# First slab behind each adaptive norm: products on h times the feature scale, token scale and shift applied in the bank afterwards

## The chip, the cores and the metric

The kernel runs on one NeuronCore of a Trainium2 chip. The metric is device time in microseconds of one execution. One core has five engines that run their own instruction streams and wait for each other by semaphores: TensorE (PE, matmul; its weight loads are PEld in the profile), VectorE (DVE), ScalarE (ACT), GpSimd (POOL) and SyncE (SP, which issues the transfers).

## The reference

Two transformer blocks run one after the other on x of 512 tokens by 1024 features, in float32. The first block has retention, forgetting attention, a cross attention to a memory and a gated feed-forward part. The second block is adaptive; what matters here is its two norms:

```
mod = silu(c) @ w_ada + b_ada;  sh1, sc1, g1, sh2, sc2, g2 = split(mod, 6)
h = rmsnorm(x, norm1_g) * (1.0 + sc1) + sh1
proj = h @ w_in                       # pool input, k, v, q
x = x + g1 * (concat(attention, pool_mixer) @ w_out)
h2 = rmsnorm(x, norm2_g) * (1.0 + sc2) + sh2
x = x + g2 * conv_gated_ffn(h2, w_up, conv_w, conv_b, w_down)
```

rmsnorm divides each token by the root of the mean of its squares over the 1024 features. So a projection behind a norm is: token scale times (weights times (h times feature scale)) plus weights times shift.

## The kernel before, in words

Everything lies with features on the 128 partitions and the 512 tokens along the free dimension, so h is 8 tiles h[:, k, :] of 128 x 512. A weight matrix is cut into slabs of 8 x 128 input features by 256 outputs (1 MB). Each float32 product is made of three products of a reduced form (fp32r): whi*xhi, whi*xlo, wlo*xhi, where xhi is the rounded value and xlo the rest. A slab has 8 k, 2 output tiles and 3 parts: 48 matmuls of 128 x 512 (three() and slab_fm(), L1366 to L1387).

A slab passes four engines. SyncE loads it into raw[s] (two buffers, s = slab number mod 2), once wlo of the slab before is made. ScalarE rounds it to whi[s] (make_hi, L408) when TensorE is done with the slab that had this buffer (slab_done). GpSimd subtracts to wlo[s] in four quarters (L388) and counts wlo_ready. TensorE waits for wlo_ready and for a pair of result banks (pair_free), and writes lin banks in turn. The results are evicted by ScalarE or VectorE.

The order of every engine is written out by hand. Around each adaptive norm it is as follows. The slabs of "down" (before norm1) or "out2" (before norm2) give four pairs of tiles; residual() on VectorE adds each to h (L1118 or L1120), residual_act() on ScalarE squares the new h (L680), and accumulate() on VectorE sums the squares in rstd (L859, L863). Then token_norm() on TensorE: one filler product into a free bank (keep_clock, L1424; a float32 product is two instructions), eight one-column products that sum the squares of each block of 128 tokens (L1433), one filler, and, when ScalarE has taken the root (L428) and VectorE the reciprocal and the scaled diagonals in tmp[0] (L872, L875), four products that spread the token scale over a bank, att[1] (L1439); then three fillers. finish_norm() then works in both engines per k: VectorE makes tmp = h * feature scale * att[1] (L887), ScalarE adds the shift and rounds to xh (L432), VectorE makes the rest xl (L881). TensorE starts k of the first slab when xl of k is there (ready, then k outside and the two tiles inside). ScalarE rounds the second slab behind the norm between the root and this loop (beside). 

Behind norm1 comes "in2" (L1735 on): ScalarE, after the loop, waits for pool["u"] (VectorE's two memsets, L1226), evicts the first slab's pair (pool_in, L744) and only then rounds the third slab (make_hi). VectorE makes window sums for the pool mixer (L1240 to L1250). Behind norm2 comes "ffn2" as a hardware loop: VectorE copies the convolution's parameters (L1325), ScalarE evicts the first slab's pair (L829), then rounds the third slab (L833), and so on.

Before norm1, VectorE also sums up the modulation (ada tiles, L1175) beside "down"; modulation() (L1207, L1211) makes the feature scales after the third pair.

## Time and profile before

| | us |
|---|---|
| median of 3 runs | 1402.72 |
| lowest, highest | 1400.03, 1402.81 |
| the profiled execution | 1399.9 |
| its span, first to last instruction | 1398.1 |
| TensorE busy | 1361.8 (97%) |
| VectorE busy | 660.2 (47%) |
| ScalarE busy | 619.4 (44%) |
| GpSimd busy | 613.9 (44%) |

Times in the profile are microseconds from the start of the span. A row of the timeline gives start, duration, engine, line of the kernel, operation, tile written and tiles read, and how often; in brackets stands how long the engine was idle before and who ended that. Merged rows (x2, x4) give the duration of the whole group. A TensorE matmul is pipelined: its duration overlaps the next, so the step is read from start to start.

### The profile page before, as it was taken

To read this page: it belongs to the slowest core of one execution; us is meant where nothing else is said; L and a number is where in the kernel's file an instruction comes from. 1 tells how busy PE (TensorE), PEld (TensorE's weight loads), DVE (VectorE), ACT (ScalarE), POOL (GpSimd) and SP (SyncE) were. 2 spreads that over 40 slices of the span, in tenths; PEclk is the share of its full clock that TensorE was granted. 3 is DMA by queue.
4 is the path that set the end of the run, shared out by engine and by line. 5 is a ranking of instruction groups with operands and counts; after the bars stand their busy time and mean duration, and the time that the engine had idled before them with its cause. 6 is when DMAs were issued, how large, how long until landed. Compare 5 with 4: busy or idle time off the path is not lost.

```text
span 1398.1 us, 17303 instructions
## 1 busy us (share of the span) xinstructions
PE 1361.8 (97%) x6544; PEld 1095.2 (78%) x6544; DVE 660.2 (47%) x973; ACT 619.4 (44%) x861; POOL 613.9 (44%) x448
## 2 busy tenths in 40 slices
PE   9999999999989999999999999988999999999999
PEld 7877955788876888888888887854878888888887
DVE  5434938355433444344343316588255555554111
ACT  5555228553444443434442123587245545554111
POOL 3444320374430456555564543411325555556453
PEclk9999999999999999999999999999999999999999
DMA  7222212142220244344436433200312222323422
GB/s 267 91 90 94 87 41 81 61 173 99 91 90 1 91 144 141 135 159 141 150 135 260 177 135 105 91 31 30 121 61 90 90 90 92 118 90 135 175 96 90
DMA packets 29055, 155.23 MB, mean 111 GB/s; under 512 B 3024, under 2 KB 4176, under 8 KB 14800
## 3 DMA queue, kind: packets, MB, share of 16 engines
q1 hardware_dynamic: 29008, 154.57, 31.5%
q8 instruction: 34, 0.56, 0.2%
q14 instruction: 13, 0.11, 0.0%
HBM read 152.46 MB, written 2.10 MB: 111 GB/s over the span
## 4 chain that ended last, share of the span: by engine, by line
issue 39%; PE 30%; POOL 26%; DVE 4%; DMA 0%; POOLq 0%; ACT 0%; SPq 0%
POOL wlo L388 26%; PE lin L1368 10%; PE lin L1370 10%; PE lin L1369 10%; DVE small L1026 1%; DVE expd L1037 1%; DMA raw<-w_slabs 0%; PE lin L1571 0%; DVE xl L906 0%; DVE win L1245 0%; DVE small L1030 0%; POOLq L397 0%; DVE wlo L914 0%; PE att L1433 0%; PE att L1439 0%
## 5 line engine op out<-in xcount | busy, mean ns | idle before, releaser
L388 POOL TENSOR_TENSOR wlo<-raw,whi 128x512 fp32r<-128x512 f32 x444 | 613.7, 1413 | 768.8 <-ACT whi L415 508.2
L1368 PE MATMUL lin<-xh,whi 128*128 128x512 f32 x1072 | 420.6, 392 | 4.0 <-POOL wlo L388 3.5
L1370 PE MATMUL lin<-xh,wlo 128*128 128x512 f32 x1072 | 417.6, 390 | 0.0
L1369 PE MATMUL lin<-xl,whi 128*128 128x512 f32 x1072 | 417.4, 389 | 0.0
L415 ACT ACTIVATE whi<-raw 128x2048 fp32r<-128x2048 f32 x66 | 126.6, 1918 | 266.7 <-PE lin L1370 260.4
L1368 PEld LDWEIGHTS lin<-xh,whi 128*128 128x128 f32 x1072 | 201.3, 188 | 52.5 <-issue 5.9
L1370 PEld LDWEIGHTS lin<-xh,wlo 128*128 128x128 f32 x1072 | 201.3, 188 | 42.1
L1369 PEld LDWEIGHTS lin<-xl,whi 128*128 128x128 f32 x1072 | 201.3, 188 | 41.4 <-issue 0.5
L1368 PE MATMUL lin<-fh,whi 128*128 128x512 f32 x352 | 137.1, 390 | 0.0
L1370 PE MATMUL lin<-fh,wlo 128*128 128x512 f32 x352 | 137.0, 389 | 0.0
L1369 PE MATMUL lin<-fl,whi 128*128 128x512 f32 x352 | 137.0, 389 | 0.0
L1368 PEld LDWEIGHTS lin<-fh,whi 128*128 128x128 f32 x352 | 66.1, 188 | 14.0 <-issue 0.3
L1370 PEld LDWEIGHTS lin<-fh,wlo 128*128 128x128 f32 x352 | 66.1, 188 | 13.6
L1369 PEld LDWEIGHTS lin<-fl,whi 128*128 128x128 f32 x352 | 66.1, 188 | 13.6
L1175 DVE CUSTOM_DVE_ANT_0 adar<-adar,c_act 128x1024 f32<-128x1024 f32 x48 | 57.9, 1215 | 38.9 <-DMA adar<-ada 38.6
L1120 DVE SCALAR_TENSOR_TENSOR h<-lin,mod,h 128x512 f32<-128x512 f32 x16 | 11.9, 751 | 118.8 <-PE lin L1370 118.8
L1331 DVE SCALAR_TENSOR_TENSOR tmp<-lin,convp,tmp 128x511 f32<-128x511 f32 x44 | 31.2, 750 | 68.4 <-ACT tmp L829 68.4
L728 ACT ACTIVATE whi<-raw 128x2048 fp32r<-128x2048 f32 x22 | 42.2, 1919 | 40.6 <-PE lin L1370 40.5
L1118 DVE TENSOR_TENSOR h<-lin,h 128x512 f32<-128x512 f32 x24 | 16.4, 691 | 86.5 <-PE lin L1370 86.4
L1184 DVE TENSOR_TENSOR tmp<-lin,rstd 128x512 f32<-128x512 f32 x22 | 15.2, 692 | 83.7 <-PE lin L1370 83.5
L1368 PE MATMUL lin<-xah,whi 128*128 128x512 f32 x128 | 50.6, 395 | 0.0
L1370 PE MATMUL lin<-xah,wlo 128*128 128x512 f32 x128 | 49.9, 390 | 0.0
(320 smaller groups left out, 1925.5 us busy)
## 6 DMA issues: line engine op xcount, KB each, us to landing
raw<-w_slabs SPq DMA_DIRECT2D x111, 1024.0 KB, 4.8
adar<-ada SPq DMA_DIRECT2D x48, 512.0 KB, 5.5
h<-x_t SPq DMA_DIRECT2D x4, 512.0 KB, 6.4
decay<-decay SPq DMA_DIRECT2D x4, 512.0 KB, 7.9
out_t<-h SPq DMA_DIRECT2D x3, 512.0 KB, 8.2
raw<-w_slabs SPq DMA_DIRECT2D x4, 256.0 KB, 7.0
rope<-rope SPq DMA_DIRECT2D x2, 512.0 KB, 7.3
memx<-mem_t SPq DMA_DIRECT2D x1, 1024.0 KB, 5.9
```

Of the source, the lines that this page charges most:

```text
L388: return nc.gpsimd.tensor_tensor(wlo[s][:, ks, :], raw[s][:, ks, :], f(whi[s][:, ks, :]), ALU.subtract)
L415: nc.scalar.activation(whi[g % 2][:, :, :], raw[g % 2][:, :, :], ACT.Copy).then_inc(whi_ready, 1)
L728: nc.scalar.activation(whi[s][:, :, :], raw[s][:, :, :], ACT.Copy).then_inc(whi_ready, 1)
L1026: last = nc.vector.tensor_reduce(ring(j, "max")[:, e:e + 1], att[n % 4][:, 0:width(j)], AX.X, ALU.max, negate=True)
L1037: nc.vector.tensor_scalar(row, row, ring(j - 1, "inverse")[:, e:e + 1], None, ALU.mult).then_inc(a["norm"], 1)
L1118: ins = nc.vector.tensor_tensor(h[:, k, :], b[:, :], h[:, k, :], ALU.add)
L1175: return nc.vector.tensor_tensor_reduce(adar[s][:, :], adar[s][:, :], c_act[:, :], 1.0, 0.0, ALU.mult, ALU.add, total).then_inc(ada["acc"], 1)
L1184: nc.vector.tensor_tensor(tmp[s][:, :], lin[2 * p][:, :], rstd[:, :], ALU.mult).then_inc(ffn["g"], 1)
L1331: nc.vector.scalar_tensor_tensor(t[:, 1:T], b[:, 0:T - 1], convp[s][:, 4 * j:4 * j + 1], t[:, 1:T], ALU.mult, ALU.add).then_inc(ffn2["tap" ...
L1368: nc.tensor.matmul(out, whi_, xhi_, start=first, stop=False)
L1369: nc.tensor.matmul(out, whi_, xlo_, start=False, stop=False)
L1370: return nc.tensor.matmul(out, wlo_, xhi_, start=False, stop=last)
```

## The change

The token scale is one factor per token, so it can be applied after the product. The first slab behind each adaptive norm is therefore multiplied with sch and scl, the high and low part of h times the feature scale, which need no token scale. For norm1 they use the memory of xh and xl (so ScalarE waits for scaled["read"] before it overwrites a tile), for norm2 free memory.

- ScalarE makes sch tiles: six in a row and the two shift copies before the last pair of "down" (norm1), or two per pair of "out2" (norm2); the last two always behind the last adds. VectorE makes scl tiles: for norm1 six behind modulation(), before the add of the last pair, and two behind the last add; for norm2 two per pair.
- TensorE's scaled_slab() replaces token_norm() and the first slab. The eight token sums stand before k = 3 and the four diagonal products before k = 6. Behind the last k stand 32 products of the 16 weight tiles (whi and wlo, two output tiles each) with a two-column operand, the high and low part of the shift. The five fillers of each norm (one, one, three) are gone.
- ScalarE rounds the second slab first, then takes the root, then copies the bank att[1] to rstd; VectorE's L887 reads rstd in place of the bank.
- VectorE's fix_slab(), within finish_norm behind k = 5, waits for the first slab, adds the two columns of the shift products, multiplies both banks in place by rstd and adds the shift sums. ScalarE (and in ffn2 VectorE) waits for scaled["fixed"] before it evicts.
- The semaphores of the second gated part are shared with the first (ffn2 uses ffn's), with offsets of FT.

```diff
+            def scaled_hi(i, k):
+                nc.scalar.activation(sch[i][:, k, :], h[:, k, :], ACT.Copy, scale=gain(i, k)
+                                     ).then_inc(scaled["hi"], 1)
             def finish_norm(n, hi, shift, beside):
+                beside()
                 act.wait_ge(n["sum"], 1)
                 nc.scalar.activation(token_root, att[0][:, 0:TT], ACT.Sqrt, bias=ccol(C_EPS)).then_inc(n["sd"], 1)
-                beside()
+                act.wait_ge(n["sum"], 2)
+                nc.scalar.activation(rstd[:, :], att[1][:, :], ACT.Copy).then_inc(n["sd"], 1)
                 for k in range(KT):
+                    if n is norms["norm1"]:
+                        act.wait_ge(scaled["read"], k + 1)
                     act.wait_ge(n["x"], k + 1)
...
@@ residual_act
+                    if norm == 0 and u == 3:
+                        act.wait_ge(ada["mod"], 1)
+                        for i in range(2):
+                            nc.scalar.activation(shift_hl[i][:, :, 0], mod[:, 3 * i * KT:(3 * i + 1) * KT], ACT.Copy
+                                                 ).then_inc(ada["shift"], 1)
+                        for k in range(6):
+                            scaled_hi(0, k)
...
+                        if norm == 1 or norm == 0 and u == 3:
+                            scaled_hi(norm, k)
...
@@ VectorE
+            def scaled_lo(i, u):
+                for k in range(2 * u, 2 * u + 2):
+                    dve.wait_ge(scaled["hi"], KT * i + k + 1)
+                    nc.vector.scalar_tensor_tensor(scl[i][:, k, :], h[:, k, :], gain(i, k), f(sch[i][:, k, :]),
+                                                   ALU.mult, ALU.subtract).then_inc(scaled["lo"], 1)
+            def fix_slab(i, p):
+                dve.wait_ge(slab_done, SLAB0["in2" if i == 0 else "ffn2"] + 1)
+                parts = att[0][:, 8:12].rearrange("p (j e) -> p j e", e=2)
+                link(nc.vector.tensor_reduce(slab_shift[i][:, :], parts, AX.X, ALU.add))
+                banks = lin[2 * (p % 2):2 * (p % 2) + 2]
+                for b in banks:
+                    last = nc.vector.tensor_tensor(b[:, :], b[:, :], rstd[:, :], ALU.mult)
+                link(last)
+                for j, b in enumerate(banks):
+                    nc.vector.tensor_scalar(b[:, :], b[:, :], slab_shift[i][:, j:j + 1], None, ALU.add
+                                            ).then_inc(scaled["fixed"], 1)
...
                 for k in range(KT):
                     if k >= 4:
                         dve.wait_ge(n["lo"], k - 3)
-                    nc.vector.scalar_tensor_tensor(tmp[k % 4][:, :], h[:, k, :], gain(k), att[1][:, :],
+                    nc.vector.scalar_tensor_tensor(tmp[k % 4][:, :], h[:, k, :], gain(i, k), rstd[:, :],
                                                    ALU.mult, ALU.mult).then_inc(n["x"], 1)
                     if k >= 1:
                         low(k - 1)
+                    if k == 5:
+                        fix_slab(i, p)
...
@@ beside_down on VectorE
                 if u == 2:
                     modulation()
+                    for i in range(2):
+                        dve.wait_ge(ada["shift"], 2)
+                        nc.vector.tensor_tensor(shift_hl[i][:, :, 1], mod[:, 3 * i * KT:(3 * i + 1) * KT],
+                                                f(shift_hl[i][:, :, 0]), ALU.subtract).then_inc(ada["shift"], 1)
+                    for v in range(3):
+                        scaled_lo(0, v)
...
@@ TensorE
+            def scaled_slab(i, name):
+                n, g, p = norms[f"norm{i + 1}"], SLAB0[name], PAIR0[name]
+                s, banks = g % 2, lin[2 * (p % 2):2 * (p % 2) + 2]
+                pe.wait_ge(wlo_ready, g + 1)
+                pe.wait_ge(pair_free, p + 1)
+                for k in range(KT):
+                    if k == 3:
...
+                                pe.wait_ge(made, count)
+                                mm = nc.tensor.matmul(att[0][:, t:t + 1], part[:, P * t:P * (t + 1)], ccol(C_MEAN_D),
+                                                      start=(e == 0), stop=(e == 1))
+                        mm.then_inc(n["sum"], 1)
+                    if k == 6:
+                        for t in range(TT):
+                            pe.wait_ge(n["inv"], t + 1)
+                            mm = nc.tensor.matmul(att[1][:, P * t:P * (t + 1)], mean_d, tmp[0][:, P * t:P * (t + 1)],
+                                                  start=True, stop=True)
+                        mm.then_inc(n["sum"], 1)
+                    pe.wait_ge(scaled["lo"], KT * i + k + 1)
+                    for j in range(2):
+                        mm = three(banks[j][:, :], whi[s][:, k, j * P:(j + 1) * P], wlo[s][:, k, j * P:(j + 1) * P],
+                                   sch[i][:, k, :], scl[i][:, k, :], k == 0, k == KT - 1)
+                    if i == 0:
+                        mm.then_inc(scaled["read"], 1)
+                pe.wait_ge(ada["shift"], 4)
+                for j in range(2):
+                    for e, w in enumerate((whi, wlo)):
+                        for k in range(KT):
+                            mm = nc.tensor.matmul(att[0][:, 8 + 2 * j:10 + 2 * j], w[s][:, k, j * P:(j + 1) * P],
+                                                  shift_hl[i][:, k, :], start=(e == 0 and k == 0), stop=(e == 1 and k == KT - 1))
+                mm.then_inc(slab_done, 1)
```

## Rows read from the trace of the kernel before

**Rows 1.** TensorE in the timeline around norm1 (start, us, engine, line, operation)

```profile
845.76 1.02 PE L1424 MATMUL c_act<-con 128*128 128x512 f32 x2
...
856.92 0.79 PE L1368 MATMUL lin<-xh,whi 128*128 128x512 f32 x1
...
868.25 0.39 PE L1368 MATMUL lin<-xh,whi 128*128 128x512 f32 x1
...
879.13 0.39 PE L1368 MATMUL lin<-xh,whi 128*128 128x512 f32 x1
```

**Rows 2.** TensorE's waits: who waited for whom, us in total, times, longest

```profile
PE lin L1368 <- POOL wlo L388: 4.9, 6, 1.4
```

**Rows 3.** TensorE in the timeline around norm2

```profile
1022.96 1.02 PE L1424 MATMUL c_act<-con 128*128 128x512 f32 x2
...
1025.76 0.36 PE L1433 MATMUL att<-con,rstd 128*128 128x1 f32 x2
1025.98 0.36 PE L1433 MATMUL att<-con,tmp 128*128 128x1 f32 x2
...
1027.76 1.92 PE L1439 MATMUL att<-tmp,con 128*128 128x128 f32 x8
...
1044.22 0.39 PE L1368 MATMUL lin<-xh,whi 128*128 128x512 f32 x1
...
1055.18 0.49 PE L1368 MATMUL lin<-xh,whi 128*128 128x512 f32 x1
```

**Rows 4.** ScalarE in the timeline around norm1

```profile
837.86 1.92 ACT L415 ACTIVATE whi<-raw 128x2048 fp32r<-128x2048 f32 x1 [8.96 <-PE lin L1370]
...
847.31 0.63 ACT L680 ACTIVATE tmp<-h 128x512 f32<-128x512 f32 x1 [4.00 <-DVE h L1118]
...
868.50 1.08 ACT L744 ACTIVATE upool<-lin 128x512 f32<-128x512 f32 x2 [3.44 <-PE lin L1370]
```

**Rows 5.** GpSimd in the timeline around norm1

```profile
839.85 5.47 POOL L388 TENSOR_TENSOR wlo<-raw,whi 128x512 fp32r<-128x512 f32 x4 [5.86 <-ACT whi L415]
...
871.47 6.66 POOL L388 TENSOR_TENSOR wlo<-raw,whi 128x512 fp32r<-128x512 f32 x4 [13.66 <-ACT whi L415]
```

**Rows 6.** ScalarE in the timeline behind norm2

```profile
1044.48 1.28 ACT L829 ACT_TABLE_LOAD   x1 [3.28 <-PE lin L1370]
```

**Rows 7.** GpSimd in the timeline behind norm2

```profile
1049.11 5.93 POOL L388 TENSOR_TENSOR wlo<-raw,whi 128x512 fp32r<-128x512 f32 x4 [15.16 <-ACT whi L833]
```

**Rows 8.** VectorE in the timeline behind norm2

```profile
1029.71 1.41 DVE L887 SCALAR_TENSOR_TENSOR tmp<-h,mod,att 128x512 f32<-128x512 f32 x2 [1.94 <-PE att L1439]
1031.25 1.56 DVE L881 SCALAR_TENSOR_TENSOR xl<-tmp,mod,xh 128x512 fp32r<-128x512 f32 x1
...
1040.37 1.62 DVE L881 SCALAR_TENSOR_TENSOR xl<-tmp,mod,xh 128x512 fp32r<-128x512 f32 x2
```

**Rows 9.** The page's groups: busy us, mean ns of one, idle before

```profile
L1184 DVE TENSOR_TENSOR tmp<-lin,rstd 128x512 f32<-128x512 f32 x22 | 15.2, 692 | 83.7 <-PE lin L1370 83.5
```

**Rows 10.** VectorE in the timeline around norm1

```profile
841.95 0.69 DVE L1118 TENSOR_TENSOR h<-lin,h 128x512 f32<-128x512 f32 x1 [24.84 <-PE lin L1370]
...
853.88 1.41 DVE L887 SCALAR_TENSOR_TENSOR tmp<-h,mod,att 128x512 f32<-128x512 f32 x2 [2.24 <-PE att L1439]
...
864.22 1.62 DVE L881 SCALAR_TENSOR_TENSOR xl<-tmp,mod,xh 128x512 fp32r<-128x512 f32 x2
...
873.60 1.68 DVE L1245 TENSOR_TENSOR win<-win 128x525 f32<-128x525 f32 x1
```

**Rows 11.** Stretches of 1 us: busy us per engine, then PEclk, DMA share, GB/s

```profile
849.00:850.00 1.00, 1.00 (x7) 1.00 (x6) 0.00 (x0) 0.00 (x0) 0.00 (x0) 0.51 1.07 275
...
855.00:856.00 1.00, 1.00 (x2) 0.34 (x1) 0.87 (x2) 1.00 (x2) 1.00 (x1) 0.57 0.08 33
...
1026.50:1027.50 1.00, 1.00 (x2) 0.27 (x1) 0.78 (x5) 1.00 (x2) 0.00 (x0) 0.51 0.00 0
...
1029.50:1030.50 1.00, 1.00 (x3) 0.50 (x3) 0.79 (x2) 0.01 (x1) 1.00 (x2) 0.78 0.00 0
```

More of the change, by code:

```diff
@@ L266, in build @@
         ffn = sems("ffn", "g act y hi lo")
-        ffn2 = sems("glu2", "pc cv tap act f hi lo")
-        ada = sems("ada", "act acc mod")
+        ffn2 = dict(ffn, **sems("glu2", "pc cv tap"))
+        scaled = sems("scaled", "hi lo read fixed")
+        ada = sems("ada", "act acc mod shift")
         pool = sems("pool", "u pooled hi lo mm")
@@ L733, in _ @@
                                          tmp[2 + s][:, :], ACT.Copy).then_inc(ffn["hi"], 1)
-            residual_act("down", norms["norm1"], 3)
+            residual_act("down", norms["norm1"], 3, norm=0)
             finish_norm(norms["norm1"], xhi, 0, lambda: make_hi(SLAB0["in2"] + 1))
@@ L742, in pool_in @@
                 act.wait_ge(pair_free, p + 2)
+                if u == 0:
+                    act.wait_ge(scaled["fixed"], 2)
                 for j in range(2):
@@ L817, in _ @@
                         beside_gqa_act, late=2)
-            residual_act("out2", norms["norm2"])
+            residual_act("out2", norms["norm2"], norm=1)
             finish_norm(norms["norm2"], xhi, 3 * KT, lambda: make_hi(SLAB0["ffn2"] + 1))
+            act.wait_ge(scaled["fixed"], 4)
             with act.Fori(0, FT // 2) as i:
@@ L867, in accumulate, with finish_norm @@
                         ins.then_inc(n["acc"], 1)
-            def finish_norm(n, gain, hi, lo, shift):
+            def scaled_lo(i, u):
[14 more added lines that the diff above has]
+                                            ).then_inc(scaled["fixed"], 1)
+            def finish_norm(i, hi, lo, p):
+                n, shift = norms[f"norm{i + 1}"], 3 * i * KT
                 dve.wait_ge(n["sd"], 1)
@@ L1092, in _, with residual @@
                                             ).then_inc(xkn["out"], 1)
-            def residual(name, n, scale=None, slabs_per_pair=1, split=None, beside=None, before=None):
+            def residual(name, n, scale=None, slabs_per_pair=1, split=None, beside=None, before=None, norm=None):
                 def low(u):
@@ L1130, in residual @@
                         beside(u)
+                if norm is not None:
+                    scaled_lo(norm, 3)
                 if split is not None:
@@ L1219, in beside_down @@
                     modulation()
+                    for i in range(2):
[4 more added lines that the diff above has]
+                        scaled_lo(0, v)
             tiles_beside_down(0)
-            residual("down", norms["norm1"], slabs_per_pair=3, beside=beside_down)
-            finish_norm(norms["norm1"], lambda k: mod[:, KT + k:KT + k + 1], xhi, xlo, shift=0)
+            residual("down", norms["norm1"], slabs_per_pair=3, beside=beside_down, norm=0)
+            finish_norm(0, xhi, xlo, PAIR0["in2"])
             link(nc.vector.memset(upool[:, :, 0:PAD], 0.0))
@@ L1317, in _ @@
             softmax_dve(gqa, 16, 4, lambda j: T, True, gqa_lo, beside_gqa_dve, late=2)
-            residual("out2", norms["norm2"], scale=lambda k: mod[:, 2 * KT + k:2 * KT + k + 1])
-            finish_norm(norms["norm2"], lambda k: mod[:, 4 * KT + k:4 * KT + k + 1], xhi, xlo, shift=3 * KT)
+            residual("out2", norms["norm2"], scale=lambda k: mod[:, 2 * KT + k:2 * KT + k + 1], norm=1)
+            finish_norm(1, xhi, xlo, PAIR0["ffn2"])
+            dve.wait_ge(scaled["fixed"], 4)
             with dve.Fori(0, FT // 2) as i:
@@ L1692, in _, with down @@
             project("ffn", slab_fm, first=2)
-            def down(name, parts):
+            def down(name, made):
                 g, p = SLAB0[name], PAIR0[name]
@@ L1732, in _ @@
             g, p = SLAB0["in2"], PAIR0["in2"]
-            for u in range(5):
+            for u in range(1, 5):
                 pe.wait_ge(wlo_ready, g + u + 1)
                 pe.wait_ge(pair_free, p + u + 1)
-                mm = slab_fm(u % 2, p + u, ready=(lambda k: pe.wait_ge(norms["norm1"]["lo"], k + 1)) if u == 0 else None,
+                mm = slab_fm(u % 2, p + u, ready=(lambda k: pe.wait_ge(norms["norm1"]["lo"], k + 1)) if u == 1 else None,
                              middle=(lambda: head_stats(2 * (u - 3))) if u >= 3 else None)
```

56 lines of the change are left out of this document (27 added, 29 removed).

## The prediction

> **What bounds the kernel now.** I read the page's busy shares first, then TensorE's waits, then the timeline around the two adaptive norms, engine by engine. TensorE is busy 97% of the span, and the split products run back to back: 48 of them, one slab, go from 868.25 to 879.13, so one takes 0.2267 us [rows 1]. What TensorE waits for by name is small: the longest total behind a slab product is 4.9 us in 6 waits, all on GpSimd's low part of the weights [rows 2]. But in two places its stream holds norm work and filler products that no wait shows. Call the slabs behind a norm A, B and C. Behind norm1 the next product could issue at 845.76 and A starts at 856.92; B starts at 868.25, where 845.76 + 10.88 would be 856.64: 11.6 us lost. Behind norm2 B starts at 1044.22, where 1022.96 + 10.88 is 1033.84: 10.4 us lost [rows 1, 3]. These 22 us are what the change can win.
>
> The reader must also see how C comes to start, since it needs whi and wlo in the buffer that A leaves. ScalarE rounds C's weights only after finish_norm's last high part, and after it has evicted A; GpSimd follows. Behind norm1 the eviction starts at 868.50, and GpSimd ends C's low part at 871.47 + 6.66 = 878.13; TensorE wants it at 879.13: slack 1.0 us [rows 1, 4, 5]. Behind norm2 the table load before the eviction starts at 1044.48, GpSimd ends at 1049.11 + 5.93 = 1055.04, and C starts at 1055.18 after B's last product: slack zero [rows 3, 6, 7]. So a later end of finish_norm on VectorE and ScalarE moves C, whatever TensorE does before it.
>
> **The change, norm2 (the simpler one).** TensorE: A's first three k (18 products, 4.1 us) run from 1022.96 to 1027.0. Then the eight token sums: a matmul of one column is two instructions, and two instructions took 0.22 us (1025.98 less 1025.76), so 1.8 us, to 1028.8 [rows 3]. Three more k: to 1032.9. Then the four diagonal products, eight instructions: 1.92 us at the lower clock [rows 3], half of it at the full one, 1.0: to 1033.9. Here is the core of my argument: before, they ran at 1027.76 and VectorE's first x (L887) began at 1029.71 [rows 3, 8]. Now A's products stand ahead of them. ScalarE must also copy the bank to rstd (0.6, the half of 1.08 and an issue, [rows 4]), so x begins at 1034.8: 5.1 later.
>
> VectorE's loop of 16 operations took 12.3 us from there (1040.37 + 1.62 less 1029.71, [rows 8]), but its first low part stood beside GpSimd and took 1.56, where two operations clear of it take 1.41, a step of 0.67 [rows 8]. Now GpSimd has converted B's weights at 1027 to 1033, so the loop is 16 such steps and the first wait for ScalarE: 11.1, a gain of 1.2. In it stands fix_slab, behind low(4): a small reduction, two multiplications and two additions over a bank. The nearest row is 0.692 for a bank times rstd [rows 9]; with two links I take 3.1 (2.7 to 3.4). Its wait for A costs nothing: TensorE ends A and the shift products by 1040.3, low(4) ends about 1042.4. Behind the wait stand x(6) and low(5), and behind these TensorE's last k of B. Sum: 5.1 - 1.2 + 3.1 = 7.0; the last low part ends at 1049.0, then convp's copy (0.17), on which the table load and the eviction wait. They start at 1049.25 instead of 1044.48: +4.8, and rounding and GpSimd follow unchanged. C starts at 1059.95. B, from 1040.3, is done at 1051.2, so TensorE stands idle some 8.7 us.
>
> The 32 shift products of two columns cost TensorE 32 x 0.11 = 3.6 us if they go like those of one column [rows 3], and 7.3 at most, at a full product each [rows 1]. Either way they are hidden: they only shorten that idle time. The five filler products go, and with them what kept TensorE in work while it waits.
>
> **Norm1.** Three things are added. (a) VectorE was idle 24.84 us before the add at 841.95 [rows 10]. Now it waits there for ScalarE's shift copies, behind the rounding of A's weights that ends at 839.8 [rows 4], and then makes six low parts. Four fall beside GpSimd's conversion from 839.85 [rows 5], where an operation with two SBUF inputs took 1.68 [rows 10] instead of 0.66 to step; so they end near 848.5, and GpSimd's own four grow to 4 x 1.66 (its 6.66 for four beside VectorE, [rows 5]): A can start at 846.5 only. The add of h[6] ends at 849.2 instead of 842.6, then three accumulations (2.1), the add of h[7] at 852.0, a scaled high part and the square on ScalarE (0.65 each, by the square's 0.63, [rows 4]): squares complete at 853.3, where before it was 847.9. TensorE has done three k at 850.6 and waits 2.7. (b) The sums end at 855.1, three k at 859.2, the diagonals at 860.2, x begins at 861.1 instead of 853.88. (c) The clock. The granted clock fell to 0.50 (1.2 GHz) from 849.0 to 855.9, after TensorE had waited and issued one-column products, and again at 1026.5 [rows 11]. Now the same thin stretch, with a longer wait, stands in the middle of A; I take 1.7 us for products that run at the lower level (0 to 4). Then +7.2 + 1.7 = 8.9 for x; the loop 0.9 shorter (no GpSimd beside it), fix_slab 3.1, and C's slack and the early end of the loop (865.84 and the memsets to 866.1, against the eviction at 868.50) take off 2.4 + 1.0. C starts 7.7 later, at 886.8; B is done by 879.
>
> **The clock at C.** In both places TensorE now stands idle 7 to 9 us before C. The trace has no idle stretch this long in mid kernel, but shorter thin ones were followed by low stretches of 6.9 and 3.4 us [rows 11]; half of 3.4 is lost if C begins in one: 1.7 each, bounds 0 and 3.4. By the Trainium skill, "TensorE: Matmul & The Clock Gate", section "Part 1: The HAM clock gate", the throttled level is the default and only activity releases it; that speaks against this change, and the rows on the granted clock agree. Without that rule the sum would be some 5 us smaller (the three clock terms).
>
> **Sum.** Norm1 7.7 + 1.7 = 9.4; norm2 4.8 + 1.7 = 6.5; together 16. From C on all engines are late alike, and the stages that follow hang on one another (slab to slab on TensorE, softmax after it), so I expect nothing back. Elsewhere the edit is free: the scaled parts of k 0 to 5 before norm2 fall into idle time of both engines between residual adds, and no DMA moves: the next weight loads wait only on wlo_ready, up to 3 us later against more than 10 of lead. The profiled execution took 1399.9 (span 1398.1), the median of the runs is 1402.72, the lowest 1400.03; 1399.9 + 16 = 1415.9, and 1417 with part of that difference.
>
> **The rivals.** *No clock loss:* everything as above without the three clock terms: +10.9, 1411 to 1413. For it: in stage norm2 the one-column products now have full ones on both sides. Against: the idle time before C is longer than any before. 22%.
>
> *The other side, TensorE's fill decides:* if ScalarE and VectorE were done in time, the change would win at B. A costs 10.9 + 1.8 + 1.0 + 3.6 (shift), plus 3.5 of waits at norm1: B at 866.5 against 868.25, and at 1040.3 against 1044.22; together -5.7, so 1394 to 1397. It decides fully from the point where C's low part is ready when B ends (877.4 and 1051.2), so where the eviction of A starts by 867.8 and 1040.6; the time is below that of before as soon as finish_norm ends no later than it did. Both need it 7 to 9 us earlier than I have it, or C's rounding ahead of the eviction. For it speaks only that 22 us lie open; I see nothing in the order of the instructions that does it. 8%.
>
> *GpSimd beside the loop:* x now reads rstd in SBUF instead of the bank, so each of its operations has two SBUF inputs. If B's weights are converted during the loop, four operations step 1.66 instead of 0.66: +4 at one norm or both, 1420 to 1425. For it: x began beside GpSimd before. Against: B's rounding is moved ahead of the root and GpSimd is done before x begins. By the skill's "SBUF — State Buffer", section "SBUF: two separate sides", such an operation and one of GpSimd exclude each other for their whole length; the 1.68 us rows agree, and by that rule x would be exposed. 8%.
>
> **How the numbers follow.** The forecast, 62%: 1417, own range 1411 to 1423 (clock terms 0 to 9, fix_slab, the stalls of norm1). With the rivals the range is 1407 to 1425. 0.2% is 2.8 us, about what a measurement of this kernel tells from no change. Faster 8% (the rival of the other side), the same 3% (my sums wrong by 13 us in between), slower 89%.
>
> **What would show it.** In the profile after: x begins near 1034.8 after norm2, not at 1029.7; TensorE's waits on wlo L388 grow from 4.9 to about 20 us, in two long ones before C; the eviction of A waits on VectorE, not on TensorE; the granted clock is 0.5 at the start of C; B starts earlier than before. Wrong would be a C that starts without a wait, or a clock that stays at 1.0 throughout, or a B that is itself late.

## The result: slower by 1.1%

| | before | after |
|---|---|---|
| median us | 1401.43 | 1415.11 |
| runs, lowest to highest | 4, 1400.03 to 1402.81 | 4, 1414.43 to 1416.34 |
| the profiled execution | 1399.9 | 1415.01 |
| its span | 1398.1 | 1412.9 |
| mean granted clock | 0.994 | 0.987 |

The ratio is 1.0107, 95% interval 1.009 to 1.0123. The forecast was 1417 (1407 to 1425).

TensorE's waits in the profile after (who waited for whom, total us, times, longest), the row that answers to [rows 2]:

```profile
PE lin L1434 <- POOL wlo L400: 16.3, 8, 5.7
```

Two waits of 5.7 and 5.6 us are new, and both are C's. TensorE's timeline behind norm1 and norm2 after, answering to [rows 1, 3]; the bracket is the idle time and who ended it:

```profile
845.75 0.47 PE L1434 MATMUL lin<-xh,whi 128*128 128x512 f32 x1
...
852.84 0.38 PE L1501 MATMUL att<-con,tmp 128*128 128x1 f32 x2 [1.49 <-ACT tmp L711]
...
855.54 0.77 PE L1434 MATMUL lin<-xh,whi 128*128 128x512 f32 x1
...
861.82 1.05 PE L1507 MATMUL att<-tmp,con 128*128 128x128 f32 x8
...
865.47 0.95 PE L1520 MATMUL att<-shift_hl,whi 128*128 128x2 f32 x8
...
868.96 0.48 PE L1434 MATMUL lin<-xh,whi 128*128 128x512 f32 x1
...
887.45 0.79 PE L1434 MATMUL lin<-xh,whi 128*128 128x512 f32 x1 [5.70 <-POOL wlo L400]
...
1032.91 0.39 PE L1434 MATMUL lin<-sch,whi 128*128 128x512 f32 x1
...
1050.05 0.49 PE L1434 MATMUL lin<-xh,whi 128*128 128x512 f32 x1
...
1068.43 0.79 PE L1434 MATMUL lin<-xh,whi 128*128 128x512 f32 x1 [5.61 <-POOL wlo L400]
...
1080.97 0.39 PE L1434 MATMUL lin<-xh,whi 128*128 128x512 f32 x1
```

A now starts at once: 845.75 instead of 856.92. B starts 0.7 later than before at norm1 (in this profile; see the first experiment), and 4.1 earlier at norm2 (1050.05 less 1044.22 is +5.8, but norm2 as a whole begins 9.95 later). Then C is 8.3 later at norm1 and, with the 9.95 taken off, 3.3 later at norm2. The slab behind C, D, shows the clock as well: it starts 13.76 and 12.54 behind C, where before it was 12.09 and 11.02. In sum D is +10.0 and then +4.8, which is the 14.8 us of the span. Up to the last product of down, from the fifth slab behind norm1 to the last product of out2, and from the fifth slab behind norm2 to the end the two profiles differ by less than 0.2 us each. So A's head start was there, and it was lost, and more, at C.

Who holds C is on the other engines. VectorE after norm1, answering to [rows 10]: the six low parts, the add of h[6], the diagonals, the x loop's first operations, the bank operations within it and the end of the loop:

```profile
841.00 7.18 DVE L905 SCALAR_TENSOR_TENSOR xl<-h,mod,xh 128x512 fp32r<-128x512 f32 x6
848.11 0.68 DVE L1173 TENSOR_TENSOR h<-lin,h 128x512 f32<-128x512 f32 x1
...
856.22 3.69 DVE L928 TENSOR_SCALAR tmp<-con,small 128x128 f32<-128x128 f32 x4
863.54 1.42 DVE L940 SCALAR_TENSOR_TENSOR tmp<-h,mod,rstd 128x512 f32<-128x512 f32 x2 [3.63 <-ACT rstd L447]
...
871.12 0.15 DVE L912 TENSOR_REDUCE slab_shift<-att 128x2 f32<-128x4 f32 x1
871.30 1.30 DVE L915 TENSOR_TENSOR lin<-lin,rstd 128x512 f32<-128x512 f32 x2
872.64 1.42 DVE L918 TENSOR_SCALAR lin<-lin,slab_shift 128x512 f32<-128x512 f32 x2
873.96 0.74 DVE L940 SCALAR_TENSOR_TENSOR tmp<-h,mod,rstd 128x512 f32<-128x512 f32 x1
...
876.88 0.75 DVE L934 SCALAR_TENSOR_TENSOR xl<-tmp,mod,xh 128x512 fp32r<-128x512 f32 x1 [0.19 <-ACT xh L453]
```

The x loop starts 9.66 us later than before, and the bank operations hold it for 2.84 (873.96 less 871.12). Behind it stand ScalarE's eviction of A and the rounding of C, then GpSimd's low part, answering to [rows 4, 5]:

```profile
877.87 1.09 ACT L777 ACTIVATE upool<-lin 128x512 f32<-128x512 f32 x2 [1.02 <-DVE upool L1292]
878.84 1.92 ACT L427 ACTIVATE whi<-raw 128x2048 fp32r<-128x2048 f32 x1
```

```profile
880.84 6.56 POOL L400 TENSOR_TENSOR wlo<-raw,whi 128x512 fp32r<-128x512 f32 x4 [21.20 <-ACT whi L427]
```

The eviction used to wait for TensorE's product; now it waits for VectorE, 9.4 us later. Norm2 after, on ScalarE, GpSimd and VectorE, answering to [rows 6, 7, 8]:

```profile
1057.10 0.72 ACT L453 ACTIVATE xh<-tmp,mod 128x512 fp32r<-128x512 f32 x1 [0.60 <-DVE tmp L940]
1057.84 1.28 ACT L862 ACT_TABLE_LOAD   x1
1059.14 1.45 ACT L862 ACTIVATE tmp<-lin,convp 128x512 f32<-128x512 f32 x2
```

```profile
1062.47 5.83 POOL L400 TENSOR_TENSOR wlo<-raw,whi 128x512 fp32r<-128x512 f32 x4 [20.42 <-ACT whi L866]
```

```profile
1044.64 1.42 DVE L940 SCALAR_TENSOR_TENSOR tmp<-h,mod,rstd 128x512 f32<-128x512 f32 x2 [2.31 <-ACT rstd L447]
...
1056.98 1.63 DVE L934 SCALAR_TENSOR_TENSOR xl<-tmp,mod,xh 128x512 fp32r<-128x512 f32 x2
1058.53 0.16 DVE L1391 COPY convp<-par 128x8 f32 x1
```

The table load stands right behind ScalarE's last high part, before VectorE's copy to convp at 1058.53 is made. The clock when C begins, in stretches of 1 us (busy us per engine, then PEclk, DMA share, GB/s):

```profile
886.00:887.00 1.00, 0.00 (x0) 0.00 (x0) 0.96 (x2) 0.00 (x0) 1.00 (x1) 0.50 0.00 0
...
888.00:889.00 1.00, 1.00 (x4) 0.76 (x3) 0.90 (x2) 1.00 (x2) 0.00 (x0) 0.50 0.54 74
...
1070.00:1071.00 1.00, 1.00 (x4) 0.81 (x3) 1.00 (x2) 1.00 (x1) 0.00 (x0) 0.50 0.75 287
```

TensorE idles at 0.50 and starts C at 0.50.

### The profile page after: what moved, and what is told of

It is laid out like the page before. It is cut to its first block, busy times and chain, and to the rows that moved or that the text cites. A ratio compares the mean times of both kernels' runs of the same rounds, so it can differ in the third digit from the quotient of the medians.

```text
span 1412.9 us, 17468 instructions
## 1 busy us (share of the span) xinstructions
PE 1366.1 (97%) x6588; PEld 1103.8 (78%) x6588; DVE 681.0 (48%) x1001; ACT 630.9 (45%) x881; POOL 613.6 (43%) x448
## 4 chain that ended last, share of the span: by engine, by line
issue 47%; POOL 28%; PE 24%; DMA 0%; DVE 0%; POOLq 0%; SPq 0%; ACT 0%
POOL wlo L400 28%; PE lin L1434 8%; PE lin L1435 8%; PE lin L1436 8%; DMA raw<-w_slabs 0%; DVE xl L961 0%; POOLq L409 0%; DVE wlo L969 0%; POOLq L412 0%; SPq L299 0%; DVE h L1175 0%; ACT xh L468 0%; SPq L305 0%; SPq L301 0%; POOLq L404 0%
## 5 line engine op out<-in xcount | busy, mean ns | idle before, releaser
L1434 PE MATMUL lin<-xh,whi 128*128 128x512 f32 x1056 | 418.0, 396 | 14.8 <-POOL wlo L400 14.8
L1434 PEld LDWEIGHTS lin<-fh,whi 128*128 128x128 f32 x352 | 66.1, 188 | 14.1 <-issue 0.3
L759 ACT ACTIVATE whi<-raw 128x2048 fp32r<-128x2048 f32 x22 | 42.2, 1920 | 40.5 <-PE lin L1436 40.4
L1243 DVE TENSOR_TENSOR tmp<-lin,rstd 128x512 f32<-128x512 f32 x22 | 15.2, 692 | 83.7 <-PE lin L1436 83.5
L1435 PE MATMUL lin<-xal,whi 128*128 128x512 f32 x128 | 49.8, 389 | 0.0
```

Source lines behind the costliest of these rows:

```text
L759: nc.scalar.activation(whi[s][:, :, :], raw[s][:, :, :], ACT.Copy).then_inc(whi_ready, 1)
L1243: nc.vector.tensor_tensor(tmp[s][:, :], lin[2 * p][:, :], rstd[:, :], ALU.mult).then_inc(ffn["g"], 1)
L1434: nc.tensor.matmul(out, whi_, xhi_, start=first, stop=False)
L1435: nc.tensor.matmul(out, whi_, xlo_, start=False, stop=False)
```

## The experiments

The theory: the time is lost where C waits for its weights' low part, because everything between the norm's sums and C's rounding stands in one order, and the sums now come later; the clock adds to it when C starts cold. Times below are medians; a ratio is to the kernel before, run beside it with a median of 1399.7 to 1400.0, and takes in all runs, so it is not the quotient of the two medians.

**Each norm alone.** Two kernels with a pair of flags: at the norm that is switched off, the old order of products, filler products, rounding and loop stands.

```diff
+ON = (True, False)        # the other kernel: (False, True)
-            scaled_slab(0, "in2")
+            scaled_slab(0, "in2") if ON[0] else token_norm(norms["norm1"])
```

> The change behind norm1 only; norm2 as before (its own first slab, fillers included). My theory (C waits for the late end of finish_norm, then starts at 1.2 GHz): in the profile the first product of the fourth in2 slab stands 10 us later than before (at about 901.2), the stretch behind norm2 is as before, the whole is 10 us over before (ratio 1.007). Rival (the loss is all in the gated part behind norm2, where the kernel is bound by one slab after another): nothing to 2 us over before. Rival (the two losses are not additive, one loss hides in the other): norm1 only plus norm2 only are not the 14 us of the whole.

> The change behind norm2 only; norm1 as before. The scaled parts of norm2 and the two small shift copies stay. My theory: the third ffn2 slab starts 3.3 us later than before relative to the end of out2, and 1.6 us more go by the lower clock: 5 us over before (ratio 1.0035). Rival (the PE's fill decides): 4 us below before, ratio 0.997.

Norm1 alone took 1409.48, ratio 1.0072 (1.0048 to 1.0097); norm2 alone 1407.22, 1.0042 (1.0023 to 1.0062). The two excesses sum to 1.14%, the whole change has 1.07%: within the intervals the norms are independent. Each shows its long wait of C unchanged:

```profile
887.62 0.80 PE L1445 MATMUL lin<-xh,whi 128*128 128x512 f32 x1 [5.74 <-POOL wlo L401]
```

```profile
1061.68 0.79 PE L1445 MATMUL lin<-xh,whi 128*128 128x512 f32 x1 [5.61 <-POOL wlo L401]
```

The first kernel also shows what is particular to the profile of the change. There the granted clock was 0.50 for 6.8 us within A (853.2 to 860.0), and B began 23.6 behind the last product of down (22.7 before). In the profile of norm1 alone, and in four more below with the same instructions up to there, it was 0.50 for 3.4 us within A, and B began 22.0 behind. So the change usually starts B 0.7 earlier at norm1 too; C then stands 40.5 behind that product and D 54.2, against 33.6 and 45.7 before: +6.9 and +8.5, where the profile of the change has +8.3 and +10.0.

**Filler products in the wait.** Eleven 512-column products of the kernel before's keep_clock stand ahead of C at both norms, to hold the clock up and change nothing else.

```diff
             for u in range(1, 5):
+                if u == 2:
+                    keep_clock(11)
                 pe.wait_ge(wlo_ready, g + u + 1)
...
+            keep_clock(11)
             project("ffn2", slab_fm, first=2)
```

> The changed kernel with 11 filler products (float32, 128 x 512, into the free bank) before the third slab behind each norm, in the time in which TensorE waits for GpSimd's low part; nothing else moves. If the low clock at C costs what I said: granted clock 1.0 when C starts, C starts when it did, the fourth slab starts 1.6 us earlier at each norm, together 3.2 us below the changed kernel, some 11.5 us over before (ratio 1.008). If the clock costs nothing of its own (something else is late behind C anyway): as the changed kernel, 14.8 over before. If the fillers themselves delay C: over 15.

It took 1419.72, ratio 1.0142 (1.0118 to 1.0165): 4.6 us above the changed kernel, where I had expected 3 below it. TensorE's row says why (22 instructions for 11 products):

```profile
880.96 9.60 PE L1490 MATMUL c_act<-con 128*128 128x512 f32 x22
...
890.00 0.80 PE L1434 MATMUL lin<-xh,whi 128*128 128x512 f32 x1
...
902.52 0.48 PE L1434 MATMUL lin<-xh,whi 128*128 128x512 f32 x1
```

A filler takes 0.87 us, so eleven overran the wait. Counted from the last product ahead of A, C stands at 42.0 instead of 40.5 at norm1 and at 39.0 instead of 35.8 at norm2. But the question of the clock is answered: C begins at full clock, and D stands 12.52 and 11.31 behind it, where the changed kernel has 13.76 and 12.54. That is 1.2 us at each norm, and it understates the cold start: behind a filler the first step of C is 0.63 us (890.00 to 890.63) instead of 0.23. Against the kernel before (12.09 and 11.02) the cold start costs 1.7 and 1.5. With six fillers:

> The changed kernel with 6 filler products before slab C at each norm. A filler took 0.87 us in the run with 11 (9.6 us together, 2 to 4 us more than the wait they stood in), so 6 take 5.2 us and fit into the 5.6 us of waiting. My theory: C starts at the same time after the end of down and out2 as in the changed kernel, C runs at the full clock, slab D starts 1.2 to 1.6 us earlier at each norm: 2.5 to 3 us below the changed kernel (ratio to before 1.008 or so). Rival (the clock's loss at C is hidden by other engines): D starts as in the changed kernel, ratio 1.010.

It took 1414.52, ratio 1.0102 (1.0085 to 1.0119). Six took 5.31 us; behind norm1 TensorE still waited 2.2 and the clock fell 0.3 us into C (D 13.81 behind it); behind norm2 C ran at full clock with D 10.99 behind it, 1.5 us won. I had expected 2.5 to 3 us for both norms together, and the time is not told apart from that of the changed kernel. So the clock was a small term: the wait has to go, not its coldness.

**Without the bank operations.** The two multiplications and two additions are left out, so the first slab lacks its token scale and shift.

```diff
-                for b in banks:
-                    last = nc.vector.tensor_tensor(b[:, :], b[:, :], rstd[:, :], ALU.mult)
-                link(last)
-                for j, b in enumerate(banks):
-                    nc.vector.tensor_scalar(b[:, :], b[:, :], slab_shift[i][:, j:j + 1], None, ALU.add
-                                            ).then_inc(scaled["fixed"], 1)
+                for j in range(2):
+                    nc.vector.tensor_copy(slab_shift[i][:, j:j + 1], slab_shift[i][:, j:j + 1]
+                                          ).then_inc(scaled["fixed"], 1)
```

> The changed kernel without the two multiplications and two additions of fix_slab over the banks (the wait for A, the small reduction and the counts stay; two copies of one element stand in for them), so the first slab behind each norm misses token scale and shift. My theory: VectorE's chain to the last low part is 2.6 us shorter at each norm and C starts that much earlier, together 5 us below the changed kernel, a little more if the clock falls later (ratio to before 1.006 to 1.007). Rival (fix_slab is hidden beside TensorE's slab B): no change.

It took 1409.53, ratio 1.0062 (1.0045 to 1.0079): 5.6 us less than the changed kernel for two times 2.8 of VectorE. C stood 16.0 and 15.2 behind B instead of 18.5 and 18.4; counted from the last product ahead of A, it is 2.5 us earlier at each norm. So VectorE's chain sets C, nearly one to one.

**C's rounding ahead of the end of the loop.** ScalarE rounds C before the seventh high part instead of behind the eviction of A.

```diff
                 for k in range(KT):
+                    if k == 6 and third is not None:
+                        make_hi(third)
...
-            with act.Fori(0, FT // 2) as i:
+            def gated_pair(i, rounded=False):
...
+            gated_pair(0, rounded=True)
+            with act.Fori(1, FT // 2) as i:
+                gated_pair(i)
```

> The changed kernel with the rounding of slab C moved into finish_norm on ScalarE, ahead of the high part of k = 6, at both norms, where ScalarE is idle 3.4 us behind fix_slab; the eviction of A no longer stands ahead of it. Simple theory (C hangs only on the order of rounding behind finish_norm): C starts when B ends, 5.7 us earlier at each norm and at full clock, together 11 to 14 us below the changed kernel, about 1402. My theory by now: GpSimd then converts beside VectorE's last five operations (steps of 1.66 for 0.66), the last low part and the eviction of A come 4 us later, and the wait moves to slab D, whose rounding stands behind that eviction: C starts 4 to 5 us earlier, D at most 1 to 2 us earlier, together 1 to 4 us below the changed kernel.

It took 1409.63, ratio 1.0066 (1.0044 to 1.0088): 5.5 us better, between the 1 to 4 of my theory and the 11 to 14 of the simple one. Counted from the last product ahead of A, C starts 6.0 us (norm1; 4.4 against norm1 alone, whose A took the same time) and 2.9 (norm2) earlier, but at norm1 the wait turns up one slab later, at D, whose low part GpSimd starts only at 893.67:

```profile
883.45 0.39 PE L1440 MATMUL lin<-xh,whi 128*128 128x512 f32 x1
...
898.82 0.80 PE L1440 MATMUL lin<-xh,whi 128*128 128x512 f32 x1 [3.03 <-POOL wlo L400]
```

Slab E stands where it stood with the change at norm1 alone (67.1 behind the last product of down in both): there, all of it is given back. At norm2 D stays 3.5 earlier.

Another 2.0 us come from something else that the edit does. To round C early behind norm2, it takes the first pass of the gated part out of ScalarE's hardware loop. In every kernel up to here each pass of that loop holds two activation table loads, in this one and in the mended kernels below none; one is left, in the pass that was taken out. The rows are of the kernel before and of the last kernel of this section:

```profile
L829 ACT ACT_TABLE_LOAD  x11: 1283/1283/1283, 1044.5 to 1264.3; - x11
L835 ACT ACT_TABLE_LOAD  x11: 1283/1283/1283, 1049.1 to 1268.9; - x11
```

```profile
L872 ACT ACT_TABLE_LOAD  x1: 1283/1283/1283, 1053.4 to 1053.4; - x1
```

TensorE's slabs in that loop step by 10.96 and 11.02 in turn with the loads and by 10.88 without, which is 1.9 to 2.0 us from the fifth slab behind norm2 to the end of the span. It has nothing to do with the token scale, and the kernel before was not run with it.

**The kernel before, without its five filler products per norm.** What did the change give up by removing them?

```diff
-                keep_clock(1)
-                keep_clock(1)
-                keep_clock(3)
```

> The kernel before without its five filler products behind each adaptive norm. If fillers only keep the clock: slabs A, B, C behind the norm begin at the lower clock for 3 to 6 us, 1 to 3 us over before at each norm (ratio 1.002 to 1.004). If the norm's small products and the wait are thin enough to drop the clock in any case: 0 to 1 us over before, or somewhat below, as the fillers themselves stand in the path (the diagonal products start after one of them).

It took 1403.28, ratio 1.0015 (1.0004 to 1.0026). At norm2 A starts 1.0 earlier without the fillers, but at the lower clock, and B 0.8 later:

```profile
1031.11 2.08 PE L1437 MATMUL att<-tmp,con 128*128 128x128 f32 x8 [0.89 <-DVE tmp L875]
1035.66 0.76 PE L1368 MATMUL lin<-xh,whi 128*128 128x512 f32 x1 [2.47 <-DVE xl L881]
```

At norm1 B came 0.9 earlier, so at the two norms together nothing is lost. What this profile has over that of before, 4.4 us of span, lies ahead of norm1, where the instructions are the same: its last product of down starts at 850.13 instead of 845.53, behind 13.7 us at the clock of 0.50 instead of 3.4. So what the fillers are worth to the old order is not shown.

**The change with its order mended.** The idea is kept. The sums are asked for after two k (one at norm2) and the diagonals after four (three) instead of three and six; ScalarE squares before it makes the scaled part, and takes the root before B's rounding; C's rounding stands ahead of the seventh high part, D's in front of the pooled tiles' parts and of the first silu.

```diff
-                    if k == 3:
+                    if k == (2, 1)[i]:            # the token sums
-                    if k == 6:
+                    if k == (4, 3)[i]:            # the diagonals' products
```

> The change kept, its order mended where my theory puts the loss. Token sums before k = 2 (norm1) or 1 (norm2) and the diagonals before k = 4 or 3; squares ahead of the scaled high parts; at norm1 only one low part ahead of h[6], with the accumulation of the third pair made earlier; ScalarE rounds B behind the root, C ahead of k = 6, D right behind A's eviction (ffn2) or behind B's results, ahead of the pooled tiles (in2). My theory: x begins about 8 to 9.5 us after the end of down and out2 instead of 17 and 12, C starts without a long wait, 3 to 5 us earlier than in the kernel before at each norm, and D is not late: 5 to 9 us below before (ratio 0.994 to 0.997). Rival (the bank work and the second set of parts cost more than the stall of TensorE, in any order): no less than before, ratio 1.000 or over.

It took 1400.87, ratio 1.0001 (0.999 to 1.0011): all 14 us are back, and nothing more, where I had expected 5 to 9 below before. One execution took 1395.58 at a mean clock of 0.998, the one with the profile; most had 0.991 to 0.993. The difference lies in low stretches elsewhere in the kernel: this profile has none ahead of norm1, that of the next kernel has 6.8 us at 251 to 258 and 3.4 us at 411 to 415, and reaches the last product of down 4.0 us later (848.20 against 844.21). So I compare distances between landmarks from here on. C stood 33.3 behind the last product of down (33.6 before) and 31.1 behind that of out2 (32.45).

C's low part had long been made at both norms. At norm2 C waited 1.4 us for A's banks, which VectorE reads last, and B had waited 0.8 for its own last low part. At norm1 it waited for neither: TensorE ran B without a break, but at the clock of 0.50 from 862.9 to 869.7, which cost 3.0 us, and C followed B's last product. The banks were evicted at 875.6. TensorE alone, in a stretch of 2 us (busy us, then PEclk, DMA share, GB/s), and C's first product:

```profile
864.00:866.00 2.00, 2.00 (x6) 0.50 0.00 0
```

```profile
877.51 0.39 PE L1448 MATMUL lin<-xh,whi 128*128 128x512 f32 x1
```

I had not seen this when I wrote the next expectation, which puts both starts of C down to the banks.

**The bank operations later in the loop.** They stand behind the eighth product of x, ahead of the last two low parts, with the memsets of upool behind them.

```diff
+                    if k == 7:
+                        fix_slab(i, p)            # and, at norm1, the two memsets
                     if k >= 1:
                         low(k - 1)
-                    if k == 5:
-                        fix_slab(i, p)
```

> The version with the order mended, and in it the two bank operations moved from behind the sixth high part to behind the eighth product of the x loop (ahead of the last two low parts), at norm1 the two memsets of upool right behind them, and at norm2 the diagonals' products one k step earlier (ahead of k = 2). In the mended version before this, C began 33.3 us behind the last product of down (13.85 us behind B, against 10.9 for 48 products) and 31.1 us behind the last of out2 (13.6 behind B), although C's low part had been done for 4.4 us at norm1 and 5.0 at norm2: it waited for A's banks, which were evicted only behind the last low part, that GpSimd's pass had slowed (1.7 us a step). Theory: with the bank operations and half of the x loop ahead of GpSimd's pass the banks come free in time; B's 48 products end 10.9 to 11.3 us behind its start and C begins 30.5 to 31 us behind the last down product and 28 to 29 behind the last of out2; the time falls by 4.5 to 5.5 us to 1395 to 1397, ratio to the kernel before 0.996 to 0.998. Rival: GpSimd's pass over C decides itself, because VectorE's steps then meet it elsewhere: the waits stay where they are within 1 us, and the time stays at 1400 to 1401. Second rival: the time is set by TensorE's clock in other parts of the kernel, and what is won at the norms does not show in the median.

> As the other kernel of this call, but the bank operations stand one step of the x loop earlier (behind the seventh product) and the diagonals' products of norm2 stay ahead of k = 3. Theory: C's banks come free about 1 us earlier at norm1, which is not needed there; the last two low parts come 0 to 1 us later, and at norm2 the loop starts 1.3 us later; time 1395.5 to 1398, within 1.5 us of the other. Rival (GpSimd's pass decides): both at 1400 to 1401.

The second kernel has the operations behind the seventh product, and norm2's diagonals after three k instead of two. They took 1399.91 and 1400.25, ratios 0.9986 (0.9974 to 0.9999) and 0.9992 (0.9981 to 1.0003): at most 2 us, where I had expected 5. In the first kernel C stands 33.2 behind the last product of down, where I had 30.5 to 31, and 30.1 behind that of out2, where I had 28 to 29. It waits at neither norm (0.4 us at norm2 in the second kernel). At norm1 there had been no wait to take away. What remained was the clock: behind the block of 32 two-column products it fell, where nothing waited. TensorE alone in the first kernel, in stretches of 2 us:

```profile
866.00:868.00 2.00, 2.00 (x20) 1.00 0.11 45
868.00:870.00 2.00, 2.00 (x11) 0.65 0.00 0
870.00:872.00 2.00, 2.00 (x6) 0.50 0.00 0
```

The block does not always do this. Nine profiles have it at norm1 and nine at norm2; in 14 of these 18 places a low stretch (3.4 us, twice 6.8) begins within the block or up to 1.5 us behind it; in four none does. One of the four is the kernel with eleven fillers, whose block at norm1 is the same and ends at 869.9:

```profile
868.00:870.00 2.00, 2.00 (x20) 1.00 0.00 0
870.00:872.00 2.00, 2.00 (x10) 1.00 0.00 0
```

**The small products spread.** The four shift products of a k step stand between its wide ones, in two banks of their own.

```diff
                     for j in range(2):
                         mm = three(banks[j][:, :], ...)
+                        for e, w in enumerate((whi, wlo)):
+                            mm = nc.tensor.matmul(att[2 + j][:, 0:2], w[s][:, k, j * P:(j + 1) * P],
+                                                  shift_hl[i][:, k, :], start=(e == 0 and k == 0), stop=(e == 1 and k == KT - 1))
```

> The last version (bank operations behind the eighth product of the x loop), and in it the 32 two-column products of the shift no longer in one block behind the slab: the four of a k step stand between its six wide products, into two banks of their own. Their count and the work of every engine stay. In the version without it the profile shows C waiting for nothing any more, but TensorE at a granted clock of 0.5 for 3 to 3.5 us behind the block of small products, at both norms (5 us slices at 0.80 and 0.77), so that B to C took 12.35 and 12.62 us against 10.9 for 48 products. Theory (the block of small products is what the clock falls on): no stretch below full clock behind A; B to C falls to 10.9 to 11.3 at both norms, the small products still cost 3.5 us in sum or a little less, and the time falls by 2.5 to 3.5 us to 1396 to 1397.5, ratio to the kernel before 0.997. Rival (the clock falls on the products of the statistics and the diagonals, or on no particular work): the low stretches stay, the time stays within 1 us of 1399.9. Second rival (a small product between wide ones waits for the wide one to drain): A takes 2 us or more longer than before, and the time rises to 1402 to 1404.

It took 1395.56 (1394.9 to 1398.02, 6 runs), ratio 0.9973 (0.9961 to 0.9985): faster than the kernel before and than the changed one. Against the version with the block (0.9986, 0.9974 to 0.9999, in another comparison) the intervals overlap, so the times alone do not show what the spreading is worth. The same stretches, and the start of B and C behind norm1:

```profile
868.00:870.00 2.00, 2.00 (x11) 1.00 0.00 0
870.00:872.00 2.00, 2.00 (x10) 1.00 0.00 0
```

```profile
868.14 0.48 PE L1448 MATMUL lin<-xh,whi 128*128 128x512 f32 x1
...
879.14 0.39 PE L1448 MATMUL lin<-xh,whi 128*128 128x512 f32 x1
```

B takes 11.0 us there, 48 products and nothing else. At norm2 there is no low stretch behind A either, but B to C takes 12.2, where I had 10.9 to 11.3: with B 1.7 us faster, the wait for A's banks is back.

```profile
1052.43 0.50 PE L1448 MATMUL lin<-xh,whi 128*128 128x512 f32 x1 [1.01 <-DVE tmp L1417]
```

That no low stretch follows the spread products rests on one profile with two places; since four of 18 places had none with the block, it is likely that the spreading did it, and not certain.

Where the 4.1 us between the profiles of before (span 1398.1) and of this kernel (1394.0) lie, counted between landmarks: from the last product of down to the fifth slab behind norm1 2.7 less, from the last product of out2 to the fifth slab behind norm2 2.2 less, from there to the end 1.9 less, and up to the last product of down 2.7 more, by low stretches (10.2 us against 3.4) in identical instructions. So the idea with its order mended is worth some 4.9 us here, and 1.9 belong to the table loads that left the gated loop. Even of the 2.2 at norm2 a part may be theirs, as one of them (1.28) stood ahead of A's eviction. A kernel before with the same loop would tell; it was not run.

## Why the prediction was right

*The sums, and with them x, come later.* Right. X began 9.66 us later at norm1 (8.9 forecast) and 5.0 at norm2 (5.1; my terms give 4.8, 0.3 of the sum has none). At norm1 the squares were complete at 852.8 (853.3), TensorE waited 2.4 (2.7), and 18 products of A then took 6.28 us instead of 4.08, with five pairs of one-column products 1.0 longer: 3.2 by the lower clock, where I had 1.7. The five other profiles of the same instructions have half of this low stretch, so the 1.7 fits the usual execution. Wrong was that GpSimd, slowed by VectorE, would hold A until 846.5: it took 5.95 us and not 6.64, and A began at 845.75. Not foreseen: the four diagonals took 3.69 and 2.95 us beside GpSimd, 0.87 in the kernel before. A's products hid it.

*The loop and the bank operations.* Right: 14.1 and 14.0 us from the first x to the end of the last low part, 14.2 forecast; 2.84 for the bank operations, 3.1 forecast. The bank-less kernel confirms that they count in full.

*C.* At norm1 +8.3 (7.7 forecast; +6.9 in the profile of norm1 alone). At norm2 +3.3, where 4.8 was forecast: the mis-sized term. I had the table load wait for the copy to convp; it started at 1057.84, right behind the last high part, beside VectorE's last two operations, and 0.85 of its 1.28 us had passed when the copy was done at 1058.69. The end of the loop came 0.4 earlier than forecast as well.

*B, a sign of being wrong.* I had named a B that is itself late. At norm1 it started 0.7 later than before, 2.5 later than my 866.5. The longer low stretch of this profile makes 1.6 us of it; in the other profiles B was 0.7 earlier than before. At norm2 it came 4.1 earlier, as forecast.

*The clock at C.* Right: 0.50 at both starts, and 1.7 and 1.5 us by D's distance against before; I had 1.7. By the Trainium skill, "TensorE: Matmul & The Clock Gate", section "Part 1: The HAM clock gate", the throttled level is the default and activity releases it; the trace agrees at C, where the clock stayed at 0.50 through the end of the wait and the first 3.2 to 3.3 us of products.

*The shift products* took 3.5 us in a block (865.47 to 868.96; 3.6 forecast), 0.11 each. That the clock would fall for 3.4 us behind them I had not considered. In the changed kernel this was hidden in B, as C waited anyway. It is one reason why TensorE's wait for wlo rose to 16.3 us and not to 20: at both norms B ended later than I had it, and at norm2 C began earlier.

*The rivals.* "TensorE's fill decides" did not hold: B came 4.1 earlier at norm2, nearly as this rival had it (3.9), and C gave it back. Its condition was right, that C's low part must be ready when B ends: the mended kernels meet it, and the last one ends at 1395.56, within the 1394 to 1397 that it named. That it lands there is partly luck: 1.9 us of it are the table loads, and the others that meet the condition stayed at 1400. "GpSimd beside the loop" did not occur in the changed kernel, for the reason given. In the mended ones it did for the last two low parts: at norm1 of the last version they took 3.07 us (the row below) where two clear of GpSimd take 1.4, and nobody waited for that; at norm2 they took 3.26, A's eviction stood behind them, and C's wait of 1.0 us followed from it.

```profile
874.46 3.07 DVE L942 SCALAR_TENSOR_TENSOR xl<-tmp,mod,xh 128x512 fp32r<-128x512 f32 x2
```

*Sum.* 14.8 us in the span against 16: norm1 10.0 (9.4), norm2 4.8 (6.5). The good fit at norm1 is helped by the longer low stretch of this profile; norm1 alone has 8.5.

## What to carry to other kernels

When work is moved ahead of a reduction to fill a wait, follow the slab after next: here the consumer of the buffers, two slabs on, was set by the same reduction through three other engines, and the head start was worth nothing until their order had been changed with it. Take the waits away one at a time and look for where each goes, and before calling a late start a wait, look whether the engine was idle at all: at norm1 it was busy at half the clock. Compare distances between landmarks, not spans, when executions of one kernel differ by as much as the change, and do so over the whole span: that is how a gain shows that belongs to a side effect of the edit, here the table loads in a loop.

## What the runs showed of the hardware

- A 512-column filler product on plain f32 takes 0.87 us (9.60 for eleven), four times the 0.227 of one split product.
- Within or behind a block of 32 two-column products at full issue the clock fell to 0.50 in 14 of 18 places, mostly for 3.4 us, with TensorE never idle; spread between wide products, the same 32 were followed by none in the two places of one profile. Spread, three wide products and one pair take 0.92 us (849.23 to 850.15 in that kernel), where three wide ones take 0.68: 0.24 a pair, 3.8 in a slab against 3.5 in a block. A as a whole took 17.3 us at norm2 either way.
- The profiles of these kernels reach norm1 behind 0 to 13.7 us of low clock although the instructions up to there are all but the same; the last product of down starts at 844.2 with none and at 850.1 with 13.7.
- Two table loads (1.28 us each) stood in each pass of ScalarE's gated loop, and none when its first pass stood ahead of the loop; TensorE's slabs there went from 10.96 and 11.02 us to 10.88.
- A tensor_scalar of 128x128 from SBUF to SBUF goes from 0.22 to 0.74 and 0.92 us (four in 0.87, 2.95 and 3.69) when it stands beside GpSimd's pass.
